# Sums of squares as rows in column groups, turned by transposes, in a two-block model on one core

## The chip, the core and the metric

The kernel runs on one core of one Trainium2 chip. Times are device microseconds of one execution. TensorE multiplies matrices into PSUM; VectorE, ScalarE and GpSimd work element by element; SyncE issues the DMAs. Each engine runs its own instructions in order and waits on semaphores.

## The reference

A first block (gated linear attention with grouped-query attention, a scan layer, two feed-forward layers) and a second block with a delta rule, latent attention and a mixture of experts, all in float32, for 256 context and 512 latent tokens of 1024 features. The two parts that the change touches, cut:

```python
# delta rule: gates of 8 heads in two directions, from 32 columns of the input projection
g = -jnp.exp(a_log) * jax.nn.softplus(alpha + dt_bias)
beta = jax.nn.sigmoid(beta_logit)
# latent attention: rms_norm(x, g) = x * rsqrt(mean(x * x) + EPS) * g
q = (rms_norm(c_q, q_a_norm_g) @ w_uq).reshape(b_, n_tok, MLA_HEADS, MLA_QK_DIM)
q = rms_norm(q, q_norm_g)                       # per head, over 128 + 64 features
kv = (rms_norm(c_kv, kv_a_norm_g) @ w_ukv).reshape(b_, n_tok, MLA_HEADS, MLA_NOPE + MLA_V)
k = rms_norm(jnp.concatenate([k_nope, k_pe], axis=-1), k_norm_g)
```

So the gates need a product of the tokens with 32 weight columns, and latent attention needs, for each token, the sum of squares over the 256 key/value features, the 64 rotary features, the 384 query features, and over each head's query.

## The kernel before

The program is a row of stages with a barrier of all engines between them. Inside a stage each engine has its own list of instructions, written out by hand in the order in which they are to run, with semaphores between the engines. There is no planner. Tokens lie in 6 tiles of 128 (two of context, four latent). `hT` holds the features on partitions, tokens along the row, in 8 slices (`KD`).

**Delta rule (`delta_mixer`).** Work goes in periods p (one head enters in each) of six steps n. In p = 0, TensorE projects the keys in step 0 (16 passes of 512 columns), the context's keys in step 1, then the gates' logits (`gate_logits`, L3609), the values in step 2 (`side("v")`, L3442), the cumulative sums of the gates (L3652, waits for `g_done`), the context's values in step 3, and the sums of squares of the keys (`ssk`, L3479). In `gate_logits` the tokens are the stationary operand (128 x 128) and the 32 gate columns `wab` the moving one: 6 tiles x 8 slices. The logits come out with tokens on partitions in `ps[:, 7]`. VectorE copies them (L3874), adds the bias, ScalarE does sigmoid (L3738), absolute value, exponential, logarithm (each with a table to load), VectorE ends with L3878 and L3879 (`g_done`). VectorE has the keys' convolution queued behind these, ScalarE has the first tap (L3683, which waits for the constants `const_in`) ahead of the gates.

**Latent attention (`mla`).** TensorE projects 8 units (keys/values, rotary key, query rank), ScalarE squares each (L4364), VectorE copies it out with its gain. Then TensorE sums the squares over the features, with the squares as the stationary operand and a column of ones (`one`) as the moving one: L4248 and L4249 for 6 tiles, L4254 for the four latent tiles. A sum comes out as one column, tokens on partitions. VectorE adds epsilon (L4491), ScalarE takes the root (L4368). Then come the rotary swap (L4258), the first keys (`keys(0)`, L4190), the second, the first values (L4201), and for each tile the turn of the scaled keys (`turn_keys`, L4211). ScalarE squares the keys of a tile at L4376 once the rotary key is rotated (`q_roped`), VectorE scales them at L4513.

The queries follow in 12 units (`lift`, L4180: six passes of 512 columns each). Behind each lift stand the sums of the unit before it (`sums`): four matmuls of one column (L4228) or, for a rotary pair, of two (L4231, with `half_ones`). Into three places the rotary swap is put, VectorE rotates (`rope`, L4480 to L4483). At the end VectorE gathers the sums (L4543 to L4545), ScalarE takes the root, and the attention itself begins with `qk(0)` and the maximum (L4560).

Each float32 matmul shows as two passes, each with its load of the stationary operand.

## Time and profile before

| | us |
|---|---|
| three runs | 4120.4, 4126.63, 4128.65 |
| median | 4126.63 |
| the profiled execution: time | 4120.5 |
| its span, first to last instruction | 4118.7 |

| engine | busy, share of the span |
|---|---|
| TensorE, matmuls | 3918.9 us, 95% |
| TensorE, loads | 2410.3 us, 59% |
| VectorE | 1656.0 us, 40% |
| ScalarE | 857.5 us, 21% |
| GpSimd | 680.1 us, 17% |

Busy time of matmuls counts pipelined passes until their modelled end. The table of stretches gives, for a part of the span, the busy time and the number of instructions of each engine and the mean granted clock of TensorE (PEclk: 1.00 is 2.4 GHz, 0.50 is 1.2 GHz).

### The profile page before, as it was taken

The numbers are of one execution on the slowest core, as the hardware profiler recorded it, in microseconds if no ns is written. First come the engines' busy times: TensorE is split into PE (matmuls) and PEld (weight loads), VectorE is DVE, ScalarE is ACT, GpSimd is POOL, SyncE is SP. The second block draws the span as 40 slices with busy tenths as digits, with TensorE's granted clock in tenths as the row PEclk, the third lists the DMA queues.
The fourth block names the chain that finished last, engine by engine and source line by source line (L and its number), as shares of the span: only waits on it lengthen the run. The fifth ranks groups of instructions, "written<-read, shape, count | busy, mean of one in ns | idle before, by whom it ended". The sixth has DMA issues, their size and how long they took to land. (4 is left out here: it accounts for less than half of the span.)

```text
span 4118.7 us, 51892 instructions
## 1 busy us (share of the span) xinstructions
PE 3918.9 (95%) x21121; PEld 2410.3 (59%) x21121; DVE 1656.0 (40%) x3076; ACT 857.5 (21%) x1680; POOL 680.1 (17%) x504
## 2 busy tenths in 40 slices
PE   7998899999999999999999999989999999999988
PEld 4565545555448666588845777767656545443333
DVE  2345343324764564443474656543244314111111
ACT  3224320000121333210113333331123201100000
POOL 0002212222420111032341423220003200000000
PEclk9999999999999999999999999999999998999999
DMA  5108611112441110164253111003300416999999
GB/s 179 41 1 286 219 41 62 62 62 100 171 129 57 47 31 26 62 255 165 92 177 68 27 32 29 22 33 113 117 1 1 164 44 256 405 421 422 422 421 372
DMA packets 323235, 580.09 MB, mean 141 GB/s; under 512 B 58828, under 2 KB 189228, under 8 KB 322360
## 3 DMA queue, kind: packets, MB, share of 16 engines
q1 hardware_dynamic: 323000, 576.77, 38.2%
q8 instruction: 170, 2.79, 0.3%
q14 instruction: 65, 0.53, 0.0%
HBM read 566.08 MB, written 10.63 MB: 140 GB/s over the span
## 5 line engine op out<-in xcount | busy, mean ns | idle before, releaser
L3442 PE MATMUL dn_ps<-room,dn_w 128*128 128x512 f32 (+1 forms) x616 | 230.8, 521 | 0.5 <-DVE dn_v_tok L3992 0.3
L974 PE MATMUL ffn_up_ps<-room 128*128 128x384 f32 (+1 forms) x704 | 203.9, 432 | 0.0
L974 PE MATMUL ffn_up_ps<-ffn_up_t,room 128*128 128x384 f32 (+1 forms) x704 | 196.7, 432 | 0.0
L5008 PE MATMUL experts_ps<-experts_ring,experts_xs 128*64 128x512 f32 (+1 forms) x768 | 162.4, 573 | 23.9 <-DMA experts_ring<-in_w_up 23.9
L2730 PE MATMUL hgrn_ps<-room,hgrn_w 128*128 128x512 f32 x372 | 170.4, 593 | 1.4 <-DVE hgrn_v L2985 0.9
L5008 PE MATMUL experts_ps<-experts_ring,room 128*64 128x512 f32 (+1 forms) x768 | 160.9, 570 | 8.7 <-DMA experts_ring<-in_w_up 8.1
L974 PEld LDWEIGHTS ffn_up_ps<-room 128*128 128x128 f32 x704 | 133.8, 190 | 55.7
L974 PEld LDWEIGHTS ffn_up_ps<-ffn_up_t,room 128*128 128x128 f32 x704 | 133.8, 190 | 55.7
L1060 DVE TENSOR_TENSOR room<-ffn_up_ps,room 128x384 f32<-128x384 f32 (+1 forms) x154 | 73.5, 489 | 222.2 <-PE ffn_up_ps L974 220.6
L5102 DVE TENSOR_TENSOR x_sb<-x_sb,experts_ps 128x512 f32<-128x512 f32 x56 | 38.5, 688 | 298.0 <-PE experts_ps L4943 298.0
L3442 PEld LDWEIGHTS dn_ps<-room,dn_w 128*128 128x128 f32 x616 | 113.0, 192 | 76.5 <-issue 67.0
L1249 PE MATMUL ffn_down_ps<-ffn_down_w_sums,ffn_w 128*128 128x512 f32 x330 | 151.7, 596 | 0.0
L5058 PE MATMUL experts_ps<-experts_ring,experts_hidT 128*64 128x512 f32 x616 | 136.9, 600 | 9.3 <-issue 5.2
L974 PE MATMUL ffn_up_ps<-room,ffn_w 128*128 128x384 f32 (+1 forms) x512 | 143.6, 434 | 0.0
L5008 PEld LDWEIGHTS experts_ps<-experts_ring,experts_xs 128*64 128x64 f32 x768 | 58.2, 140 | 129.0 <-issue 126.6
L664 PE MATMUL out_ps<-out_w,room 128*128 128x512 f32 x296 | 130.7, 600 | 0.8 <-ACT room L712 0.8
L974 PEld LDWEIGHTS ffn_up_ps<-room,ffn_w 128*128 128x128 f32 x512 | 96.9, 190 | 41.4 <-issue 1.1
L5008 PEld LDWEIGHTS experts_ps<-experts_ring,room 128*64 128x64 f32 x768 | 54.1, 139 | 110.2 <-issue 109.1
L1249 PEld LDWEIGHTS ffn_down_ps<-ffn_down_w_sums,ffn_w 128*128 128x128 f32 x330 | 63.5, 192 | 80.6 <-issue 79.4
L5058 PEld LDWEIGHTS experts_ps<-experts_ring,experts_hidT 128*64 128x64 f32 x616 | 51.1, 138 | 90.6 <-issue 90.4
L3829 POOL TENSOR_TENSOR dn_LT<-dn_W,cst 128x384 f32<-128x384 f32 x48 | 48.0, 1000 | 331.9 <-DVE dn_W L3915 294.8
L2730 PEld LDWEIGHTS hgrn_ps<-room,hgrn_w 128*128 128x128 f32 x372 | 65.8, 191 | 60.7 <-issue 59.4
(707 smaller groups left out, 7318.2 us busy)
## 6 DMA issues: line engine op xcount, KB each, us to landing
experts_ring<-in_w_gate SPq DMA_DIRECT2D x128, 704.0 KB, 15.3
experts_ring<-in_w_up SPq DMA_DIRECT2D x128, 704.0 KB, 17.0
experts_ring<-in_w_down SPq DMA_DIRECT2D x160, 512.0 KB, 14.1
att_wm<-in_mod_w SPq DMA_DIRECT2D x20, 2048.0 KB, 9.6
ffn_w<-in_ffn_w_down SPq DMA_DIRECT2D x37, 1024.0 KB, 4.9
ffn_up_wm<-in_ada_w SPq DMA_DIRECT2D x12, 2048.0 KB, 12.6
ffn_w<-in_ffn_w_up SPq DMA_DIRECT2D x22, 1024.0 KB, 7.6
ffn_front<-in_ffn_w_down SPq DMA_DIRECT2D x18, 1024.0 KB, 4.8
```

The costliest lines, as they stand in the source:

```text
L664: mm = nc.tensor.matmul(ps[:, u % BANKS, 0:wd], xT[:, k, t * P:(t + 1) * P], wt[:, j % ring, k, 0:wd], start=k == 0, stop=k == kt - 1)
L974: mm = nc.tensor.matmul(result(n, p), lhs[:, k, :], rhs[:, k, :], start=k == 0, stop=k == half - 1)
L1060: nc.vector.tensor_tensor(kept(n, to), result(n, p), kept(n, q), ALU.add).then_inc(done, 1)
L1249: mm = nc.tensor.matmul(result(p, prod), lhs, rhs, start=j == 0, stop=j == STEPS - 1)
L2730: mm = nc.tensor.matmul(ps[:, bank, :], weights(j, k)[:, piece * P:(piece + 1) * P], hT[:, k, CTX:], start=k == 0, stop=k == KD - 1)
L3442: mm = nc.tensor.matmul(out, ahead.tile[:, k, :] if k < by_ahead else wt[:, h % 2, piece, k, :], hT[:, k, tok], start=k == 0, stop=k == KD ...
L3829: nc.gpsimd.tensor_tensor(LT[:, :, :], W[:, h % 2, :, :], small(SMALL_HALVES + n + 1), ALU.mult).then_inc(S["lt_done"], 1)
L5008: mm = nc.tensor.matmul(ps[out_rows, 3 * n + c, 0:b - a], xs_now[:, j, at:at + SLOTS], ring[:, w_at + a:w_at + b], start=j == 0, stop=j == ...
L5058: mm = nc.tensor.matmul(ps[out_rows, 6 + half, :], hidT[:, f, out_rows], ring[:, w_at:w_at + 512], start=f == 0, stop=f == FT - 1)
L5102: nc.vector.tensor_tensor(dst, dst, ps[:, bank, :], ALU.add).then_inc(S["scatter_out"], 1)
```

## The change

The operands of the sums trade places. In latent attention the squares become the moving operand. The stationary one is a window of `marks`, 32 columns wide, that is one in the column of the head's row and zero elsewhere, so that each head's sum lands in its own row. Each token tile (or pair of tiles) has its own group of 32 output partitions. The sums come out as rows, with tokens along the row: three groups of 256 tokens for keys/values and rotary key, four of 128 for the queries' rank and for the queries themselves. The query sums of all 12 units add up in the same place. ScalarE (first sums) or VectorE (queries) copies the rows to SBUF, TensorE turns them by transposes, and VectorE reads them with tokens on partitions as before. The gates' logits are made in the same way: `wab` is stationary, three groups of 256 tokens, one ScalarE copy, two transposes set into the values' projection. The transposes of the first sums stand between the first and the second keys, and VectorE waits for them; the query rows are turned after the last rotary swap. GpSimd sets the marks with nine memsets in place of one, and the constant `half_ones` with its DMA goes.

Semaphore names, the width of `marks` and the loop over the constants' DMAs are left out here.

```diff
@@ -3328,13 +3328,16 @@
         wab = spare[:, 2 * (SPAN + GAP):][:, 0:KD * 4 * H].rearrange("p (k n) -> p k n", k=KD)
+        AB_GROUPS, AB_TOK = 3, 2 * P
+        AB_ROWS = AB_GROUPS * 4 * H
+        ab_rows = dec[0:AB_ROWS, 0:2, :].rearrange("p c i -> p (c i)")
         n_ahead = ahead.tile.shape[1]
...
@@ -3602,11 +3605,19 @@
             side_a = (None, "kc", "v", "vc", None, "kk")
-            def gate_logits():
+            def gate_rows():
+
                 pe.wait_ge(S["ab_in"], 16)
-                for c in range(TILES):
-                    for k in range(KD):
-                        mm = nc.tensor.matmul(ps[:, 7, c * 4 * H:(c + 1) * 4 * H], hT[:, k, c * P:(c + 1) * P], wab[:, k, :], start=k == 0, stop=k == KD - 1)
+                for k in range(KD):
+                    for n in range(AB_GROUPS):
+                        mm = nc.tensor.matmul(ps[n * 4 * H:(n + 1) * 4 * H, 6, 0:AB_TOK], wab[:, k, :], hT[:, k, n * AB_TOK:(n + 1) * AB_TOK], start=k == 0, stop=k == KD - 1)
+                mm.then_inc(S["ab_rows"], 1)
+
+            def gate_tokens():
+
+                pe.wait_ge(S["ab_rows_out"], 1)
+                for c in range(AB_TOK // P):
+                    mm = nc.tensor.transpose(ps[:, 7, c * AB_ROWS:(c + 1) * AB_ROWS], ab_rows[:, c * P:(c + 1) * P], ident[0:AB_ROWS, 0:AB_ROWS])
                 mm.then_inc(S["ab_mm"], 1)
@@ -3619,12 +3630,16 @@
                     side("q", hp, 0, KD // 2)
+                elif p == 0 and n == 2:
+                    side("v", hp, 0, 2)
+                    gate_tokens()
+                    side("v", hp, 2, KD)
                 else:
                 if p == 0 and n == 1:
-                    gate_logits()
+                    gate_rows()
                 if n == 0:
@@ -3774,6 +3789,9 @@
                     raw("kc", hp)
+                    if p == 0:
+                        act.wait_ge(S["ab_rows"], 1)
+                        nc.scalar.copy(ab_rows, ps[0:AB_ROWS, 6, 0:AB_TOK]).then_inc(S["ab_rows_out"], 1)
                     tap0("k", hp)
@@ -3871,7 +3889,7 @@
             dve.wait_ge(S["const_in"], CONSTS)
-            nc.vector.tensor_copy(ab[:, :, :].rearrange("p c j -> p (c j)"), ps[:, 7, 0:TILES * 4 * H]).then_inc(S["ab_out"], 1)
+            nc.vector.tensor_copy(ab[:, :, :].rearrange("p (n c) j -> p n c j", n=AB_GROUPS), ps[:, 7, 0:TILES * 4 * H].rearrange("p (c n j) -> p n c j", n=AB_GROUPS, j=4 * H)).then_inc(S["ab_out"], 1)
             dve.wait_ge(S["ab_out"], 1)
@@ -4119,7 +4137,19 @@

-        CONSTS = 16 * 12 + 1
+        CONSTS = 16 * 11 + 4
+        GROUP = P // 4
+        FIRST_GROUPS, FIRST_TOK = 3, 2 * P
+        FIRST_ROWS = FIRST_GROUPS * GROUP
+        kv_rows, cq_rows, q_rows = qn[0:FIRST_ROWS, 0, 0:FIRST_TOK], qn[:, 1, 0:P], cT[:, 0, 0:P]
+
+        def whole_mark(r, rows=slice(0, P)):
+
+            return marks[rows, 0, H - 1 - r:H - 1 - r + GROUP]
+
+        def pair_mark(r):
+
+            return marks[:, 1, 2 * H - 2 - r:2 * H - 2 - r + GROUP]

@@ -4223,12 +4253,9 @@
                 src = q_sq[:, ring_slot[u], :]
-                if what == "qn":
-                    for c in range(LATENT):
-                        mm = nc.tensor.matmul(ps[:, 6, c * H + n:][:, 0:1], src[:, c * P:(c + 1) * P], one[:, 2:3], start=True, stop=True)
-                else:
-                    for c in range(LATENT):
-                        mm = nc.tensor.matmul(ps[:, 6, (LATENT + c) * H + 2 * n:][:, 0:2], src[:, c * P:(c + 1) * P], one[:, 0:2], start=True, stop=True)
+                mark = whole_mark(n) if what == "qn" else pair_mark(H + 2 * n)
+                for c in range(LATENT):
+                    mm = nc.tensor.matmul(ps[c * GROUP:(c + 1) * GROUP, 6, 0:P], mark, src[:, c * P:(c + 1) * P], start=u == FIRST_Q, stop=u == len(units) - 1)
                 mm.then_inc(S["ss_mm"], 1)
@@ -4242,22 +4269,26 @@
             pe.wait_ge(S["squares"], sq_through[4])
-            for c in range(TILES):
-                tok = slice(c * P, (c + 1) * P)
-                for i in range(KC):
-                    nc.tensor.matmul(ps[:, 4, c:c + 1], sqc[:, i, tok], one[:, 2:3], start=i == 0, stop=i == KC - 1)
-                mm = nc.tensor.matmul(ps[:, 4, 8 + c:9 + c], kp[0:ROPE, 3, tok], one[0:ROPE, 2:3], start=True, stop=True)
+            for i in range(KC + 1):
+                for n in range(FIRST_GROUPS):
+                    tok = slice(n * FIRST_TOK, (n + 1) * FIRST_TOK)
+                    lhs, rhs = (whole_mark(0), sqc[:, i, tok]) if i < KC else (whole_mark(1, slice(0, ROPE)), kp[0:ROPE, 3, tok])
+                    mm = nc.tensor.matmul(ps[n * GROUP:(n + 1) * GROUP, 4, 0:FIRST_TOK], lhs, rhs, start=i == 0, stop=i == KC)
             mm.then_inc(S["ss_mm"], 1)
             pe.wait_ge(S["squares"], sq_through[7])
-            for c in range(LATENT):
-                for i in range(KQ):
-                    mm = nc.tensor.matmul(ps[:, 6, 16 + c:17 + c], sqq[:, i, c * P:(c + 1) * P], one[:, 2:3], start=i == 0, stop=i == KQ - 1)
+            for i in range(KQ):
+                for c in range(LATENT):
+                    mm = nc.tensor.matmul(ps[c * GROUP:(c + 1) * GROUP, 6, 0:P], whole_mark(0), sqq[:, i, c * P:(c + 1) * P], start=i == 0, stop=i == KQ - 1)
             mm.then_inc(S["ss_mm"], 1)
             keys(0)
+            pe.wait_ge(S["rows_out"], 2)
+            for c in range(FIRST_TOK // P):
+                nc.tensor.transpose(ps[:, 4, FIRST_TOK + c * FIRST_ROWS:FIRST_TOK + (c + 1) * FIRST_ROWS], kv_rows[:, c * P:(c + 1) * P], ident[0:FIRST_ROWS, 0:FIRST_ROWS])
+            nc.tensor.transpose(ps[:, 6, P:2 * P], cq_rows, ident).then_inc(S["first_turned"], 1)
             keys(1)
@@ -4277,6 +4308,8 @@
             swap_q(PAIRS - 1)
+            pe.wait_ge(S["q_rows_out"], 1)
+            nc.tensor.transpose(ps[:, 6, P:2 * P], q_rows, ident).then_inc(S["q_turned"], 1)

@@ -4393,6 +4426,10 @@
                 square(u)
+            act.wait_ge(S["ss_mm"], 1)
+            nc.scalar.copy(kv_rows, ps[0:FIRST_ROWS, 4, 0:FIRST_TOK]).then_inc(S["rows_out"], 1)
+            act.wait_ge(S["ss_mm"], 2)
+            nc.scalar.copy(cq_rows, ps[:, 6, 0:P]).then_inc(S["rows_out"], 1)
             root(1, sm[:, 1, 0:TILES], sm[:, 0, 0:TILES])
@@ -4441,7 +4478,13 @@
         def _(pool):
-            nc.gpsimd.memset(one[:, 2:3], 1.0).then_inc(S["const_in"], 1)
+            for n, part, value in ((0, slice(0, H - 1), 0.0), (0, slice(H - 1, H), 1.0), (0, slice(H, GROUP + H - 1), 0.0),
+                                   (1, slice(0, 2 * H - 2), 0.0), (1, slice(2 * H, GROUP + H - 1), 0.0)):
+                nc.gpsimd.memset(marks[:, n, part], value).then_inc(S["marked"], 1)
+            pool.wait_ge(S["marked"], 5)
+            for a in range(2):
+                for b in range(2):
+                    nc.gpsimd.memset(marks[a * ROPE:(a + 1) * ROPE, 1, 2 * H - 2 + b:2 * H - 1 + b], 1.0 if a == b else 0.0).then_inc(S["const_in"], 1)
             for u in range(len(unit_list)):
@@ -4487,16 +4530,20 @@
                 evacuate(u)
-            dve.wait_ge(S["ss_mm"], 1)
-            nc.vector.tensor_scalar(sm[:, 0, 0:TILES], ps[:, 4, 0:TILES], 1.0 / KV_RANK, EPS, ALU.mult, ALU.add).then_inc(S["small"], 1)
-            own(nc.vector.tensor_scalar(sm[:, 10, 0:TILES], ps[:, 4, 8:8 + TILES], 1.0 / MLA_DH, EPS, ALU.mult, ALU.add))
+            dve.wait_ge(S["first_turned"], 1)
+            by_group = ps[:, 4, FIRST_TOK:FIRST_TOK + 2 * FIRST_ROWS].rearrange("p (c n r) -> p n c r", c=2, n=FIRST_GROUPS)
+
+            def grouped(x):
+                return x.rearrange("p (n c) -> p n c", c=2)
+
+            nc.vector.tensor_scalar(grouped(sm[:, 0, 0:TILES]), by_group[:, :, :, 0], 1.0 / KV_RANK, EPS, ALU.mult, ALU.add).then_inc(S["small"], 1)
+            own(nc.vector.tensor_scalar(grouped(sm[:, 10, 0:TILES]), by_group[:, :, :, 1], 1.0 / MLA_DH, EPS, ALU.mult, ALU.add))
             dve.wait_ge(S["evac"], evac_through[4])
             own(nc.vector.scalar_tensor_tensor(sm[:, 11, 0:TILES], sm[:, 2, 0:TILES], 1.0 / MLA_DH, sm[:, 2, 0:TILES], ALU.mult, ALU.mult))
-            dve.wait_ge(S["ss_mm"], 2)
-            own(nc.vector.tensor_scalar(sm[:, 10, 8:8 + LATENT], ps[:, 6, 16:16 + LATENT], 1.0 / Q_RANK, EPS, ALU.mult, ALU.add))
+            own(nc.vector.tensor_scalar(sm[:, 10, 8:8 + LATENT], ps[:, 6, P:2 * P].rearrange("p (c r) -> p c r", r=GROUP)[:, :, 0], 1.0 / Q_RANK, EPS, ALU.mult, ALU.add))
             own(nc.vector.tensor_scalar(sm[:, 10, 8:8 + LATENT], sm[:, 10, 8:8 + LATENT], EPS, None, ALU.mult))
@@ -4540,8 +4587,11 @@
             HQ = LATENT * H
-            own(nc.vector.tensor_copy(sm[:, 4, 0:HQ], ps[:, 6, 0:HQ]))
-            own(nc.vector.tensor_tensor(sm[:, 3, 0:HQ], ps[:, 6, HQ:2 * HQ], sm[:, 4, 0:HQ], ALU.add))
+            nc.vector.tensor_copy(q_rows, ps[:, 6, 0:P]).then_inc(S["q_rows_out"], 1)
+            dve.wait_ge(S["q_turned"], 1)
+            q_sums = ps[:, 6, P:2 * P].rearrange("p (c r) -> p c r", r=GROUP)
+            own(nc.vector.tensor_copy(by_tile(sm[:, 4, 0:HQ]), q_sums[:, :, 0:H]))
+            own(nc.vector.tensor_tensor(by_tile(sm[:, 3, 0:HQ]), q_sums[:, :, H:2 * H], by_tile(sm[:, 4, 0:HQ]), ALU.add))
             nc.vector.scalar_tensor_tensor(by_tile(sm[:, 3, 0:HQ]), by_tile(sm[:, 3, 0:HQ]), 1.0 / MLA_DH, over_heads(sm[:, 10, 8:8 + LATENT], LATENT), ALU.mult, ALU.add).then_inc(S["small"], 1)
```

## Rows read from the trace of the kernel before

**Rows 1.** Stretches around the gates; the columns are named in the first line.

```profile
core 0: us, PE busy (x) PEld busy (x) DVE busy (x) ACT busy (x) POOL busy (x), PEclk, DMA share, GB/s
...
2210.10:2226.20 16.10, 16.10 (x98) 16.06 (x97) 0.00 (x0) 4.09 (x5) 0.50 (x1) 0.66 0.81 143
...
2242.00:2246.20 4.20, 4.20 (x6) 1.66 (x7) 3.95 (x7) 2.05 (x3) 3.44 (x2) 0.59 0.23 69
```

**Rows 2.** Timeline around the gates: start, duration, engine, line, operation, idle before it.

```profile
2210.12 16.14 PEld L3609 LDWEIGHTS dn_ps<-x_sb,room 128*128 128x128 f32 x96
...
2220.29 0.94 ACT L3683 ACTIVATE dn_kT<-x_sb,dn_taps 128x772 f32<-128x772 f32 x1 [9.38 <-DMA dn_dtb<-in_dt_bias]
...
2222.77 1.28 ACT L3738 ACT_TABLE_LOAD   x1
...
2227.12 0.28 ACT L3738 ACTIVATE dn_beta<-dn_ab 128x96 f32<-128x96 f32 x1 [3.06 <-DVE dn_gx L3876]
...
2231.17 0.26 DVE L3879 SCALAR_TENSOR_TENSOR dn_g<-dn_g,dn_al 128x96 f32<-128x96 f32 x1
...
2234.47 1.43 PE L3652 MATMUL dn_ps<-dn_g,cst 128*128 128x48 f32 x12
...
2240.07 1.50 PE L3479 MATMUL dn_ps<-cst,dn_sq 128*128 128x1 f32 x12 [0.64 <-ACT dn_sq L3704]
```

**Rows 3.** Stretches of latent attention's first sums and of what follows them.

```profile
2979.40:2991.10 11.70, 11.70 (x62) 11.24 (x61) 0.99 (x3) 2.09 (x3) 0.00 (x0) 0.66 0.00 0
2991.10:2998.40 7.30, 7.30 (x12) 3.17 (x13) 2.67 (x7) 0.00 (x0) 0.00 (x0) 0.60 0.01 3
```

**Rows 4.** Timeline from the first sums to the first turn of keys.

```profile
2979.87 0.50 PE L4248 MATMUL mla_ps<-mla_one,mla_probs 128*128 128x1 f32 x4
...
2991.16 2.05 PE L4258 MATMUL mla_ps<-mla_kr,cst 128*128 128x512 f32 x2
...
2993.36 0.69 DVE L4480 TENSOR_TENSOR mla_probs<-mla_ps,mla_sin 128x512 f32<-128x512 f32 x1 [6.99 <-PE mla_ps L4258]
...
2998.57 1.02 ACT L4376 ACTIVATE mla_probs<-mla_ps 128x1024 f32<-128x1024 f32 x1 [12.03 <-PE mla_ps L4190]
...
3002.02 1.22 DVE L4513 TENSOR_TENSOR mla_probs<-mla_ps,mla_sm 128x1024 f32<-128x1024 f32 x1
...
3005.84 1.09 PE L4211 MATMUL mla_ps<-cst,mla_probs 128*128 128x128 f32 x8
```

**Rows 5.** Timeline of the query units and of their end.

```profile
3054.41 0.95 PE L4228 MATMUL mla_ps<-mla_one,mla_probs 128*128 128x1 f32 x8
...
3057.88 0.95 PE L4231 MATMUL mla_ps<-mla_one,mla_probs 128*128 128x2 f32 x8
...
3091.34 0.19 DVE L4543 COPY mla_sm<-mla_ps 128x32 f32<-128x32 f32 x1
...
3098.41 0.96 DVE L4560 TENSOR_REDUCE mla_st<-mla_ps 128x1 f32<-128x768 f32 x1 [3.21 <-PE mla_ps L4298]
```

**Rows 6.** Timeline of the modulation's matmuls in column groups and their neighbours.

```profile
1777.85 1.89 PE L974 MATMUL ffn_up_ps<-room 128*128 128x256 f32 x8
1779.67 3.68 PE L1005 MATMUL ffn_up_ps<-ffn_up_wm,conditions 128*2 128x128 f32 x128
1783.28 3.72 PE L974 MATMUL ffn_up_ps<-room,ffn_w 128*128 128x256 f32 x16
1786.84 3.62 PE L974 MATMUL ffn_up_ps<-ffn_up_t,room 128*128 128x256 f32 x16
1790.29 1.89 PE L974 MATMUL ffn_up_ps<-room 128*128 128x256 f32 x8
...
323.75 1.64 PEld L2176 LDWEIGHTS att_ps<-att_wm,conditions 128*2 128x2 f32 x64 [1.47 <-DMA att_wm<-in_mod_w]
...
325.61 1.16 PEld L2226 LDWEIGHTS att_ps<-even_raw 64*128 64x128 f32 x8 [0.22 <-issue]
```

**Rows 7.** Loads, grouped by line and shape: busy us, mean ns of one.

```profile
L3442 PEld LDWEIGHTS dn_ps<-room,dn_w 128*128 128x128 f32 x616 | 113.0, 192 | 76.5 <-issue 67.0 <-DVE dn_neg_m L3969 0.5 <-DVE dn_v_tok L3992 0.4
L1005 PEld LDWEIGHTS ffn_up_ps<-ffn_up_wm,conditions 128*2 128x2 f32 x768 | 19.4, 85 | 3.6 <-issue 3.0
```

More of the change, by code:

```diff
@@ L3211, in rope_tables @@
         pick[2 * c:2 * c + 2, c, :] = two.T
-    tables = {"rope_cos": np.cos(ang), "rope_sin": np.sin(ang), "rope_swap": swap, "half_ones": two, "pick_rows": pick}
+    tables = {"rope_cos": np.cos(ang), "rope_sin": np.sin(ang), "rope_swap": swap, "pick_rows": pick}
     return {name: np.ascontiguousarray(t.astype(np.float32)) for name, t in tables.items()}
@@ L3336, in delta_mixer @@
         ps = stack.enter_context(nc.psum_tensor(f"{tag}_ps", [P, 8, 512], F32))
-        block, S = stack.enter_context(phase(nc, tag, "const_in", "ab_in", "triangle_in", "w_in*6", "ab_mm", "ab_out", "gates", "gates_act", "g_done", "sums_mm", "sums_exp", "neg_done",
+        block, S = stack.enter_context(phase(nc, tag, "const_in", "ab_in", "triangle_in", "w_in*6", "ab_rows", "ab_rows_out", "ab_mm", "ab_out", "gates", "gates_act", "g_done", "sums_mm", "sums_exp", "neg_done",
                                              "side", "y_mm", "d_mm", "dt_mm", "ks_mm", "tr_mm", "su_mm", "o_mm",
@@ L4058, in mla @@
         sm = sb("sm", 12, 48)
-        one = sb("one", 3)
+        marks = sb("marks", 2, P // 4 + H - 1)
         st = sb("st", 2, 4, 2)
@@ L4075, in mla @@
         ps = stack.enter_context(nc.psum_tensor(f"{tag}_ps", [P, 8, 512], F32))
-        block, S = stack.enter_context(phase(nc, tag, "const_in", "up_in*2", "mm_done", "squares", "evac", "v_out", "ss_mm", "small", "root", "swapped", "rotated",
+        block, S = stack.enter_context(phase(nc, tag, "const_in", "up_in*2", "mm_done", "squares", "evac", "v_out", "ss_mm", "rows_out", "first_turned", "q_rows_out", "q_turned", "marked", "small", "root", "swapped", "rotated",
                                              "kr_turned", "kr_copied", "v_mm", "k_mm", "k_squared", "k_sum", "k_mean", "k_root", "k_scaled", "k_turned", "k_out", "kp_out", "q_roped", "scores", "top_done", "max_done", "exp_done", "inverted",
@@ L4108, in _ @@
                 sp.dma_start(cols[rows, GAIN_KP:GAIN_KP + 1], k_gain[NOPE:].rearrange("(p a) -> p a", a=1)).then_inc(S["const_in"], 16)
-            for dst, src in ((cos, "quarter_cos"), (sin, "quarter_sin"), (swap, "quarter_swap"), (one[:, 0:2], "half_ones")):
-                sp.dma_start(dst if src in ("quarter_swap", "half_ones") else dst[:, :], I[src]).then_inc(S["const_in"], 16)
+            for dst, src in ((cos, "quarter_cos"), (sin, "quarter_sin"), (swap, "quarter_swap")):
+                sp.dma_start(dst if src == "quarter_swap" else dst[:, :], I[src]).then_inc(S["const_in"], 16)
             kv = w_ukv.rearrange("(k p) (h f) -> p k h f", p=P, h=H)
```

## The prediction

> **What bounds the kernel now.** I read the table of busy shares first: TensorE is busy in almost the whole span, every other engine in less than half of it, so what counts is TensorE's time in its own program order, wherever no other engine holds it up. Then I looked for the lines that the diff removes and found each in the timeline, and I read the granted clock around them in the table of stretches. Three places come out.
>
> The gates' logits: 96 passes (48 matmuls, each two passes in float32) between 2210.1 and 2226.2 us [rows 2]. The reader is to see the granted clock beside it: 0.66 in that stretch, that is, it falls from 2.4 to 1.2 GHz while these passes run, whose moving operand is 32 columns wide [rows 1].
>
> Latent attention's first sums: 36 + 24 passes with one moving column from 2979.87 us to the swap at 2991.16 us [rows 4], 11.3 us. The clock again falls under them (0.66) and stays down over the dense passes behind them (0.60) [rows 3].
>
> The query sums: eight passes of one or two moving columns between each two lifts. From 3054.41 to 3057.88 us one period takes 3.47 us [rows 5]. Its lift is six passes of 512 columns. A pass of 256 columns takes 0.216 us: sixteen of them lie between 1786.84 and 1790.29 us [rows 6]. So 512 columns take 0.43, the lift 2.59, and the sums 0.88 us.
>
> **What a group of columns costs.** The kernel already has such matmuls: the modulation writes four groups of output partitions, each matmul with 128 moving columns. In the gate and up projections 128 such passes go from first load to the next line's first load in 3.61 us, in the attention stage 64 in 1.86 us [rows 6]. The difference of 64 passes is 1.75 us, 27 ns a pass or 0.109 us for a round of four, which is what one pass of 128 columns takes alone (half of 0.216). So four groups run side by side. The rest of 3.61 us is 0.11. Entering costs 0.10 more (eight passes before it take 1.82 instead of 1.73 us) and leaving 0.11 (sixteen take 3.56 instead of 3.45). So a block is its rounds plus 0.32 us of switching. The new stationary operand is 32 columns wide, not 2. A load of 2 columns takes 85 ns, one of 128 192 ns [rows 7]; I take about 110 ns by their spacing, which shows at a block's head only (0.03), since four loads of 32 columns are what one load of 128 is, and those keep up with 128 moving columns today. If they did not overlap the streams, each round would be twice as long; I keep that for a rival.
>
> The Trainium skill, page "TensorEngine Tiling (Array Packing)", section Key Properties, says that a change of the tiling mode drains TensorE, and this change puts 24 such changes among the query lifts. By that rule, the trace agrees: the 0.32 us is such a drain. The page gives no price of its own. The Trainium skill, page "TensorE: Matmul & The Clock Gate", section on packing small matmuls, gives 2.38 times for three column tiles, where the rounds here are counted as three at once. By it the two blocks with three groups would take a quarter longer, 1.2 us in all, and 0.9 of that is in the gates, where it is hidden.
>
> **Part 1, gates.** 24 matmuls, 48 passes of 256 columns in three groups: 16 rounds x 0.216 + 0.32 = 3.8 us in place of 16.1. TensorE comes to the values' projection at 2213.9 instead of 2226.2 us. But who waits for the gates? ScalarE cannot start its part before the convolution's taps are in: it waits for that DMA until 2220.29 us, then loads a table until 2224.05 us [rows 2]. The chain from its sigmoid at 2227.12 to the end of the logarithm's last step on VectorE at 2231.43 us is 4.31 us. In the new order the logits are there at about 2216 (rows out by ScalarE, two transposes inside the values' projection), so the sigmoid starts at 2224.05 and the gates are done at 2228.4, 3.1 us earlier. TensorE has finished the values by 2213.9 + 6.9 + 0.4 = 2221.2 and now waits for the gates until 2228.4; 12.3 us of saved passes become about 7 us of idle time. Behind it stand the cumulative sums, the context's values and the sums of the keys' squares, which before started at 2240.07 us, held up by ScalarE's square [rows 2]. That square hangs on the convolution, which VectorE has queued behind the gates, so it moves by 3.1 us. TensorE wakes up at half clock: 12 passes of 0.2 and 16 of 0.43 (twice their time at full clock) put it at 2237.7 us, at full clock at 2234.5; the square is ready at 2237.0. So this part gives 2.4 to 3.1 us there. What the clock does next is open: before, the queries' passes ran at 0.59 [rows 1], about 1.7 us lost. If that goes, it is 4.8; if another 1.7 comes, 0.7. I take 3.0. ScalarE's new copy lies in a stretch where it only waits for the taps.
>
> **Part 2, first sums.** Keys' and values' sums: 9 matmuls, 18 passes of 256 columns, six rounds of 0.216 = 1.29 us. The queries' rank: 12 matmuls, 24 passes, six rounds of 0.109 = 0.65. Switching 0.32 and 0.2 for the two changes between them (64 rows for the rotary part, then four groups; an estimate from the 0.10 of entering). Together 2.5 in place of 11.3: 8.8 us. If the clock stays up, the ten passes of the swap and the first keys take 4.6 us to their reader instead of 7.41 (2991.16 to 2998.57) [rows 4]: 2.8 us more. Against it, three transposes ahead of the second keys: 0.5 us with their gaps. Together 11.1 us.
>
> That is TensorE's order alone. The new waits: ScalarE's two copies stand ahead of its root, TensorE's transposes behind the first keys; the copies end by about 2983, the transposes stand at 2986.7, so nobody waits. VectorE's first small steps now wait for the transposes (2987.2), and the rotation of the rotary keys is queued behind them. Its three operations of 0.69 us [rows 4] end at 2989.9, and only then may ScalarE square the keys. From there to the scaled keys it is 4.67 us (2998.57 to 3003.24), so 2994.6. TensorE reaches the turns at 2987.2 + 6.9 + 0.6 = 2994.7, against 3005.84 before. There is next to no slack, and a microsecond may be lost here. Bounds for this part: 9 (loads and chain dearer) and 12.
>
> **Part 3, query sums.** 2 rounds x 0.109 + 0.32 + 0.03 = 0.57 in place of 0.88 us, 0.31 x 11 = 3.4 us. The twelfth block is covered by VectorE's rotation. Bounds: 0 (a block costs what it did) and 6 (switching costs next to nothing). At the end VectorE copies the rows out, TensorE turns them and VectorE goes on: about 0.8 us later than at 3091.34, and the rotation of the last pair behind it. Before the first maximum VectorE idles 3.21 us [rows 5], which hides it; without that cover it would cost the 0.8.
>
> **The rest.** Nine memsets in place of one on GpSimd, and eleven constants instead of twelve from the queue of SyncE, lie at the stage's start, under the first projections: 0. The stages follow each other with barriers and the experts' weights are requested after them, so the gain is kept.
>
> Sum: 3.0 + 11.1 + 3.4 = 17.5 us. The profiled execution took 4120.5 us (span 4118.7, 1.8 around it), near the fastest of the three; the median is 6.1 above. Against the execution it gives 4103, against the median 4126.63 - 17.5 = 4109.
>
> **Rivals.**
> (a) The gates give nothing, because TensorE idles and the clock takes back the rest: 14.5 us gained, 4112. For it: the new idle time of 7 us; against it: before, this stretch has half clock too.
> (b) The drains eat part 3 (a block costs 0.88): 14.1 gained, 4112.5. For it: VectorE and ScalarE are not the limit, so each drain is on the path; against it: the 0.32 measured between dense blocks [rows 6]. This is the mechanism the tiling page warns of.
> (c) With 32 columns to load, groups do not run side by side. First sums: 18 x 0.216 + 24 x 0.109 + 0.5 = 7.0, so 4.5 less than forecast. A query block is 8 x 0.109 + 0.35 = 1.2, 0.3 worse than before. The gates' logits take 10.7 us and still end near 2221, which hides it. 3.0 + 6.6 - 3.6 = 6.0 gained, 4120.6, within what can't be told from no change.
> (d) Slower: each group's matmul must drain the array before the next, so that a query block of eight passes costs 0.4 us each, 3.2 us: 2.3 x 11 = 26 lost, and the first sums with 42 x 0.4 = 17 us lose 5.5 more. Half of that comes back at the clock and the gates, 6: about 25 slower, 4152. It decides from 2.2 us a block on. Against it: 27 ns a pass in 64 and in 128 passes [rows 6].
>
> **How the numbers follow.** Forecast 0.65, (a) 0.13, (b) 0.12, (c) 0.08, (d) 0.02. A measurement of this kernel tells about 0.2%, 8.3 us, from no change. Faster by more than that: the first three, 0.90; within it: 0.08; slower: 0.02. The range takes the bounds of the parts (0.7 to 4.8, 9 to 12, 0 to 6), about 9.7 to 22.8 gained, and a few microseconds for the runs, which spread over 8: 4101 to 4118.
>
> **What would show it.** In the profile after: 48 passes of the rows within 4 us of 2210; TensorE idle before the cumulative sums, with the gates done near 2228; the granted clock at 1.00 through the first sums; the scaled keys ready when TensorE arrives; a query period of 3.16 us. The prediction fails if a query block stays near 0.9 us, if the clock falls after the first sums, or if TensorE waits for the scaled keys.

## The result and the profile after

| | median us | lowest to highest | runs |
|---|---|---|---|
| before | 4119.42 | 4114.13 to 4128.65 | 6 |
| after | 4097.82 | 4090.99 to 4105.98 | 6 |

The ratio is 0.9948, with a 95% interval of 0.9938 to 0.9958: 21.6 us faster. The forecast was 4109, 17.5 below a median of 4126.63, with a range of 4101 to 4118; the time fell out of that range at the lower end. The profiled execution of the changed kernel took 4105.98 us, the slowest of its six. So its span (4104.2) against that of before (4118.7) shows less than the runs do.

The page of the changed kernel, busy times:

```profile
PE 3905.2 (95%) x21061; PEld 2383.8 (58%) x21061; DVE 1656.4 (40%) x3077; ACT 857.2 (21%) x1683; POOL 679.7 (17%) x512
```

TensorE has 13.7 us less to do; the other engines are as they were.

**Gates.** Stretches of the changed kernel: the logits' rows, the idle time ahead of the cumulative sums, from these to the keys' sums of squares, and what follows:

```profile
2209.20:2212.83 3.63, 3.63 (x49) 1.88 (x49) 0.00 (x0) 0.37 (x1) 0.00 (x0) 1.00 0.76 5
2220.20:2228.10 7.90, 0.01 (x1) 0.01 (x1) 1.18 (x5) 7.77 (x12) 0.50 (x1) 0.78 0.79 237
2228.10:2236.30 8.20, 8.20 (x29) 7.17 (x29) 6.14 (x4) 4.43 (x5) 4.34 (x2) 0.58 0.00 0
2236.30:2250.00 13.70, 12.54 (x49) 7.23 (x49) 11.77 (x14) 7.02 (x8) 6.02 (x3) 1.00 0.15 40
```

Its timeline there:

```profile
2209.24 3.17 PEld L3613 LDWEIGHTS dn_ps<-room,x_sb 128*32 128x32 f32 x48 [0.33 <-issue]
...
2214.65 0.33 PE L3620 MATMUL dn_ps<-cst,dn_dec 96*128 96x96 f32 x2
...
2223.72 0.28 ACT L3753 ACTIVATE dn_beta<-dn_ab 128x96 f32<-128x96 f32 x1
...
2227.78 0.26 DVE L3897 SCALAR_TENSOR_TENSOR dn_g<-dn_g,dn_al 128x96 f32<-128x96 f32 x1
...
2228.09 2.79 PE L3667 MATMUL dn_ps<-dn_g,cst 128*128 128x48 f32 x12 [7.93 <-DVE dn_g L3897]
...
2235.25 0.85 ACT L3719 ACTIVATE dn_sq<-dn_kT 128x772 f32<-128x772 f32 x1
...
2236.30 1.40 PE L3482 MATMUL dn_ps<-cst,dn_sq 128*128 128x1 f32 x12
```

The reader is to see four things. The 48 passes take 3.6 us instead of 16.1 [rows 1]. TensorE then idles 7.9 us, since the gates are ready only at 2228.04. It comes back at 1.2 GHz (0.58 in the third stretch). And from the keys' sums of squares on the clock is 2.4 GHz (1.00), where before it was down again for part of the stretch behind them [rows 1].

**First sums and first keys:**

```profile
2974.50:2977.00 2.50, 2.50 (x44) 1.19 (x43) 0.75 (x1) 0.96 (x2) 0.00 (x0) 1.00 0.00 0
2977.00:2989.00 12.00, 12.00 (x39) 5.45 (x35) 6.07 (x14) 3.87 (x7) 0.00 (x0) 1.00 0.01 1
```

```profile
2974.61 1.06 PE L4276 MATMUL mla_ps<-mla_probs,mla_marks 128*32 128x256 f32 x12
...
2976.16 0.86 PE L4281 MATMUL mla_ps<-mla_probs,mla_marks 128*32 128x128 f32 x24
...
2976.95 1.12 PE L4285 MATMUL mla_ps<-mla_kr,cst 128*128 128x512 f32 x2
...
2981.35 0.33 PE L4290 MATMUL mla_ps<-cst,mla_qn 96*128 96x96 f32 x2
...
2983.42 0.69 DVE L4526 TENSOR_TENSOR mla_kr<-mla_probs 128x512 f32<-128x512 f32 x1
...
2984.21 1.02 ACT L4409 ACTIVATE mla_probs<-mla_ps 128x1024 f32<-128x1024 f32 x1 [1.98 <-DVE mla_kr L4526]
...
2987.66 1.22 DVE L4560 TENSOR_TENSOR mla_probs<-mla_ps,mla_sm 128x1024 f32<-128x1024 f32 x1
...
2989.11 1.09 PE L4241 MATMUL mla_ps<-cst,mla_probs 128*128 128x128 f32 x8
```

The sums take 2.34 us to the swap instead of 11.29, at full clock; swap to first turn takes 12.15 us instead of 14.68 [rows 3, 4]. The keys are scaled at 2988.88 and TensorE arrives at 2989.11, so no wait has come in.

**Query units:**

```profile
3034.30 0.42 PE L4258 MATMUL mla_ps<-mla_probs,mla_marks 128*32 128x128 f32 x8
3034.66 2.84 PE L4210 MATMUL mla_ps<-mla_cqT,mla_big 128*128 128x512 f32 x6
3037.43 0.43 PE L4258 MATMUL mla_ps<-mla_probs,mla_marks 128*32 128x128 f32 x8
```

A period is 3.13 us (3034.30 to 3037.43) instead of 3.47 [rows 5].

### The profile page after: what moved, and what is told of

Read it like the earlier page. It is cut to its first block and busy times, and to the rows that moved or that the text cites. A ratio compares the mean times of both kernels' runs of the same rounds, so it can differ in the third digit from the quotient of the medians.

```text
span 4104.2 us, 51781 instructions
## 1 busy us (share of the span) xinstructions
PE 3905.2 (95%) x21061; PEld 2383.8 (58%) x21061; DVE 1656.4 (40%) x3077; ACT 857.2 (21%) x1683; POOL 679.7 (17%) x512
## 5 line engine op out<-in xcount | busy, mean ns | idle before, releaser
L5058 PEld LDWEIGHTS experts_ps<-experts_ring,experts_xs 128*64 128x64 f32 x768 | 59.2, 140 | 126.8 <-issue 123.8
## 6 DMA issues: line engine op xcount, KB each, us to landing
experts_ring<-in_w_down SPq DMA_DIRECT2D x160, 512.0 KB, 13.7
```

The source lines that it names most:

```text
L5058: mm = nc.tensor.matmul(ps[out_rows, 3 * n + c, 0:b - a], xs_now[:, j, at:at + SLOTS], ring[:, w_at + a:w_at + b], start=j == 0, stop=j == ...
```

## The experiments

The kernels were run in three groups, each on a chip of its own, and beside each group the kernel before was timed on the same chip: 4119.65 us (33 runs) beside the first four kernels, 4120.62 (22) beside the next four, 4118.84 (16) beside the last four.

### One part at a time

Each of three kernels is the kernel before with one part of the change; a fourth is the kernel before itself, timed as if it were a new one. A theory or a rival below is named as in the expectation that stands ahead of the run.

```diff
 # gates alone: the hunks in delta_mixer
-                    gate_logits()
+                    gate_rows()
 # first sums alone: rows, copies and transposes of L4276 to L4291, queries as before
-                    nc.tensor.matmul(ps[:, 4, c:c + 1], sqc[:, i, tok], one[:, 2:3], ...)
+                    mm = nc.tensor.matmul(ps[n * GROUP:(n + 1) * GROUP, 4, 0:FIRST_TOK], lhs, rhs, ...)
 # queries alone
-                        mm = nc.tensor.matmul(ps[:, 6, c * H + n:][:, 0:1], src[:, c * P:(c + 1) * P], one[:, 2:3], ...)
+                    mm = nc.tensor.matmul(ps[c * GROUP:(c + 1) * GROUP, 6, 0:P], mark, src[:, c * P:(c + 1) * P], ...)
```

Gates alone. 

> The kernel before with the gates' part alone. Theory A, the parts add up and each is worth what its own stretch of the trace shows: the delta rule's stage 4.2 us shorter (3.0 if the clock falls again at the queries' passes), the other stages as before; by the clock about 4 us faster, ratio 0.9990. Rival B, the gates are only worth something together with the rest: 0 to 1 us in the stage. The whole change was 21.6 us faster by its medians and 17.6 by the stages of its trace; A puts the difference down to runs, B to one of the parts.

First sums alone. 

> Latent attention's first sums alone as rows in groups. Theory A: from the first sum to the first turn of keys 14.5 us instead of 26.0, so 11.4 us, ratio 0.9972. Rival B (the part is worth more by the clock than the trace shows, because a clock that stays up helps beyond its stretch): over 15 us faster.

Query sums alone. 

> The queries' sums alone as rows in groups. Theory A: a period of lift and sums 3.13 us instead of 3.47, 3.7 us over the eleven, less up to 1 us at the turn at the end (a transpose at half clock ahead of the first scores): 3 us faster, ratio 0.9993. Rival B: over 7 us faster, or none at all if the drains cost more where the rest is unchanged.

The kernel before. 

> The kernel before, not changed at all. Theory A: run to run the times spread over 10 us, since the granted clock falls in other places of each execution, and medians of five such runs differ by up to 4 us (ratio 0.999 to 1.001). Rival B (runs of one kernel agree, so a difference of 4 us between two medians has a cause in the program): within 1 us.

| kernel | median us | ratio | 95% interval |
|---|---|---|---|
| gates | 4115.89 | 0.9988 | 0.9978 to 0.9997 |
| first sums | 4112.03 | 0.9980 | 0.9969 to 0.9991 |
| query sums | 4117.00 | 0.9992 | 0.9983 to 1.0001 |
| the kernel before | 4117.60 | 1.0000 | 0.9990 to 1.0010 |

In microseconds of 4119.5: 4.9, 8.2 and 3.3, together 16.5, each known to about 4 and the sum to about 7. All three came out as their theory A has it, within that. The gates' interval only just leaves out no change, and the queries' does not; their stretches are clearer. From the delta rule's first matmul to the solve's first the gates alone make 59.2 us into 54.2. The unchanged kernel shows what single executions scatter: 4109.83 to 4127.47 over eleven, with a median 2.05 us below that of the 33 beside it, as its theory A has it.

### The whole change again, with padding, without column groups, and with the waits moved

The whole change again. 

> The whole change once more, with more runs. Theory A (what it is worth is what the changed stretches of the traces show, 17 to 18 us, and the 21.6 of the first six runs had luck in it): ratio 0.9957, 18 us faster. Rival B (21.6 us is its true worth, and 4 us come from somewhere that the stretches don't show): ratio 0.9948 again, with an interval that leaves 0.9957 out.

It took 4096.56 us, ratio 0.9943 (0.9929 to 0.9957). Theory A's 0.9957 lies at the very end of the interval, so that the median speaks for rival B, but does not leave A out.

The first sums padded: ten dense matmuls of 512 columns (twenty passes, no output of theirs is used) ahead of the rotary swap.

```diff
             pe.wait_ge(S["evac"], evac_through[4])
+            keep_busy(nc, ps[:, 7, :].rearrange("p (a n) -> p a n", a=4), ident, ident.unsqueeze(1).broadcast_to([P, 4, P]), 10)
             nc.tensor.matmul(ps[:, 7, :], swap, kr...)
```

> The whole change, with ten dense matmuls of 512 columns (the identity, result unused) between the first sums and the rotary swap, so that this stretch takes as long as before but with a busy array. Theory A, the first sums gave by two means, 8.4 us by fewer passes and 2 by a clock that stays up behind them: the stretch to the swap 10.9 us again, the stretch from the swap to the first turn 12.15 us as in the change, against 13.3 to 14.7 with the sums of before; 9 us slower than the whole change. Rival B, the clock is off the path there, the stretch behind the swap is what the new order of waits makes it: no difference to be seen at the clock, which would be 1.00 in both, and the stretch from the swap longer than 12.15 or the stretch before it not 10.9.

It took 4112.73 us, ratio 0.9980 (0.9970 to 0.9991). Stretches of the padded kernel, from its sums to the swap and on to the first turn:

```profile
2978.10:2989.20 11.10, 11.10 (x63) 5.05 (x63) 0.75 (x1) 2.51 (x4) 0.00 (x0) 1.00 0.00 0
2989.20:3001.30 12.10, 12.10 (x37) 5.46 (x35) 6.07 (x14) 2.46 (x5) 0.00 (x0) 1.00 0.00 1
```

The padded sums are as long as those of before (11.03 against 11.29 us from the first sum to the swap), but TensorE is fed with wide operands, and behind them the clock stays at 1.00: swap to turn takes 12.06 us, not 14.68. So the part's gain behind the swap (2.5 us in the profiled executions) is the clock, and comes from what runs in the sums and not from how long they take: theory A. The other 8.9 us (11.29 less 2.34) are the sums themselves; part of these too is clock, since they ran at 0.66 before [rows 3] and run at 1.00 now. By the medians the padding costs 16 us, where theory A had 9 and its twenty passes take 8.6. The two ratios (15 us apart, known to about 7) leave room for that, and the open point below comes back to it.

The query sums without column groups: one matmul of 512 columns a unit, and four transposes at the end instead of one.

```diff
-                for c in range(LATENT):
-                    mm = nc.tensor.matmul(ps[c * GROUP:(c + 1) * GROUP, 6, 0:P], mark, src[:, c * P:(c + 1) * P], start=u == FIRST_Q, stop=u == len(units) - 1)
+                mm = nc.tensor.matmul(ps[0:GROUP, 6, :], mark, src, start=u == FIRST_Q, stop=u == len(units) - 1)
```

> The whole change, but the queries' sums in one group of 32 rows: per unit one matmul of 512 moving columns (two passes) in place of four of 128 (eight passes), turned by four transposes. It does the same sums. Theory A, four groups run side by side and the rest of a block is the switch: two passes of 0.43 and 0.32 make 1.2 us, the period 3.8 us in place of 3.13, 7 us slower than the whole change. Rival B, a block's cost is a price for each pass or the drain, not the streaming: two passes cost no more than eight, the period stays at 3.13 us or below.

It took 4107.97 us, ratio 0.9964 (0.9950 to 0.9978). Its timeline:

```profile
3036.12 1.05 PE L4257 MATMUL mla_ps<-mla_probs,mla_marks 128*32 128x512 f32 x2
3037.10 2.84 PE L4210 MATMUL mla_ps<-mla_cqT,mla_big 128*128 128x512 f32 x6
3039.87 1.04 PE L4257 MATMUL mla_ps<-mla_probs,mla_marks 128*32 128x512 f32 x2
```

The period is 3.75 us, 0.62 more than with groups and 0.28 more than before; theory A had 3.8. From the first lift to the last rotary swap it is 48.74 us, against 41.93 with groups and 45.67 before. In the query units, trading the operands alone makes the kernel slower: two passes of 512 tokens past 32 columns take 1.05 us in these rows, the two past 128 columns of the rotary swap 1.12 us above. There, only four streams side by side turn it into a gain. The first sums and the gates were not run without groups.

The waits moved: VectorE convolves the first keys before the last two steps of the gates, TensorE projects the context's values ahead of the wait for `g_done`, and four dense passes stand ahead of the last rotary swap.

```diff
                     side("v", hp, 2, KD)
+                    side("vc", hp)
...
+            for j in range(1, DN_CONV):
+                conv("k", 0, j)
             dve.wait_ge(S["gates_act"], 5)
...
             sums(len(units) - 1)
+            keep_busy(nc, ps[:, 4, :].rearrange("p (a n) -> p a n", a=4), ident, ident.unsqueeze(1).broadcast_to([P, 4, P]), 2)
             swap_q(PAIRS - 1)
```

> The whole change, and three moves in the stretches where engines wait now: VectorE does the first keys' convolution while ScalarE makes the gates (it was queued behind them), TensorE projects the first context values before it waits for the gates, and two dense matmuls (identity, unused) stand ahead of the last rotary swap. Theory A, after the change the way to the first ssk is the chain gates, convolution, silu, square and no longer TensorE: ssk 3 us sooner, and the attention's first scores up to 1.5 us sooner if the clock stays up; 4 us faster than the whole change, ratio to before 0.9946 or so. Rival B, TensorE's own order is the path there all the same: no change at ssk, and the added matmuls only cost.

It took 4100.72 us, ratio 0.9951 (0.9937 to 0.9965), not distinguishable from the whole change and not the 4 us faster that theory A had. Its timeline and stretches behind the gates:

```profile
2233.33 2.80 PE L3668 MATMUL dn_ps<-dn_g,cst 128*128 128x48 f32 x12 [5.23 <-DVE dn_g L3912]
...
2237.88 0.85 ACT L3707 ACTIVATE dn_kT<-dn_kT 128x772 f32<-128x772 f32 x1
2238.76 0.85 ACT L3720 ACTIVATE dn_sq<-dn_kT 128x772 f32<-128x772 f32 x1
...
2239.66 2.72 PE L3482 MATMUL dn_ps<-cst,dn_sq 128*128 128x1 f32 x12 [3.54 <-ACT dn_sq L3720]
```

```profile
2233.30:2239.60 6.30, 2.80 (x12) 2.63 (x12) 0.00 (x0) 4.54 (x6) 2.92 (x2) 0.50 0.00 0
2239.60:2246.00 6.40, 6.09 (x16) 4.15 (x17) 3.29 (x8) 3.98 (x6) 2.44 (x2) 0.50 0.01 3
2246.00:2260.00 14.00, 13.10 (x41) 6.42 (x39) 10.42 (x10) 4.25 (x5) 5.03 (x4) 0.99 0.14 36
```

The square of the keys now ends 6.3 us after the gates (2239.61 against 2233.27), in the changed kernel 8.1, since ScalarE no longer waits for the convolution. But the context's values no longer cover the time until then. TensorE idles twice, 5.2 and 3.5 us, and stays at 1.2 GHz (0.50) up to 2246, through the sums of squares and most of the projection behind them, where the changed kernel has 1.00. From the stage's first matmul to the sums of squares it took 36.42 us against 37.54 in the changed kernel, 1.1 less where 3 were expected; from there to the solve's first (L3496) 20.35 against 17.24. Together that is 56.77 against 54.78. Less waiting at one place was paid back at the clock. The dense passes ahead of the last swap show nothing: the stretch behind it took 14.4 us at 1.00, as in three traces without them.

### Three pairs and the whole

The parts alone summed to 16.5 us and the whole was measured at 21.6 and 24. So all three pairs were run, with the whole once more.

> The whole change once more, beside its three pairs. The parts alone gained 4.9 (gates), 8.2 (first sums) and 3.3 us (query sums) by their ratios, 16.5 in all, each known to about 4 us; the whole gained 21.6 and 24. Theory 1, the parts simply add and the whole was measured somewhat high: about 4102, ratio 0.9958. Theory 2, the whole is worth more than its parts alone: about 4097, ratio 0.9945 again.

> First sums and query sums as rows, the gates as before. Theory 1 (parts add): 11.5 by the parts' ratios to 14.5 by the forecast's own sum, ratio 0.9972 to 0.9965. Theory 2 (these two parts, in one stage, lift each other by the clock): 19 us or more, ratio 0.9954 or below, and the whole then stands only some 3 us below it.

> Gates and first sums as rows, the query sums as before. Theory 1: 13 to 14 us gained, ratio about 0.9967, and the whole is 3.4 us below it, which is what the query units' own rows give (eleven times 0.34). Theory 2: more than 18 us, or the whole more than 6 us below it.

> Gates and query sums as rows, the first sums as before. Theory 1: 6.4 to 8 us gained, ratio about 0.9982, and the whole is 10 to 12 us below it (the forecast priced the first sums at 11.1). Theory 2: the whole is 15 us or more below it.

| kernel | median us | ratio | 95% interval |
|---|---|---|---|
| whole | 4096.52 | 0.9945 | 0.9931 to 0.9958 |
| first sums and queries | 4107.49 | 0.9970 | 0.9959 to 0.9982 |
| gates and first sums | 4103.07 | 0.9960 | 0.9947 to 0.9972 |
| gates and queries | 4111.39 | 0.9979 | 0.9970 to 0.9987 |

All eight combinations are now there, so each part can be taken in four settings. By the ratios, in us of 4119.5 (whole: mean of its three ratios, 22.5):

| part | alone | beside the one | beside the other | beside both | mean | by the traces |
|---|---|---|---|---|---|---|
| gates | 4.9 | 8.2 (first sums) | 5.4 (queries) | 10.1 | 7.2 | 4.8 |
| first sums | 8.2 | 11.5 (gates) | 9.1 (queries) | 13.9 | 10.7 | 10.2 |
| queries | 3.3 | 3.7 (gates) | 4.1 (first sums) | 6.0 | 4.3 | 3.7 |

A mean is known to about 3 us (half-widths near 0.001 of 4119.5, eight ratios in two fours, taken as independent). The last column is the difference of stretches between fixed instructions. From the delta rule's first matmul to the solve's first (L3496 in the changed kernel) it is 59.16 to 59.20 us in the five traces with the old logits and 53.88 to 54.86, mean 54.4, in the eight with the new ones (the kernel with the waits moved, 56.77, left out). From the first sum to the first turn it is 14.50 us in all the traces with the new sums that are not padded; in the five with the old ones 25.97 (the profiled execution of before), 24.45, 24.40, 24.34 and 24.29, mean 24.7. From the first lift to the last rotary swap it is 45.67 and 41.93.

The pairs do not settle between the two theories. The whole itself came out where theory 2 had it, at 0.9945, with theory 1's 0.9958 at the end of its interval. First sums with queries gave 11.3 us by the medians, as theory 1 had it, and their interval leaves out the 19 of theory 2. But the whole stands 11.0 us below them, 6.6 below gates with first sums and 14.9 below gates with queries, each more than theory 1 had. None of the intervals, of parts, pairs or whole, excludes that the means simply add. The three ratios of the whole together, as independent, put it at 22.5 us give or take 3, which is more than the 16.5 of the parts alone; but that sum is itself known to about 7 only. The traces' column adds to 18.7; the 3.5 us that the runs show beyond it are about what a mean is known to.

Part of it has a place. Stretches from the last rotary swap to the third `qk` in the changed kernel, in the whole change as run last, and before:

```profile
3071.00:3088.70 17.70, 14.40 (x47) 7.18 (x47) 8.34 (x20) 4.78 (x9) 2.62 (x1) 0.81 0.00 0
```

```profile
3070.90:3085.30 14.40, 11.08 (x47) 5.98 (x47) 8.37 (x20) 4.77 (x9) 2.63 (x1) 1.00 0.00 0
```

```profile
3091.40:3107.40 16.00, 12.66 (x46) 6.73 (x46) 8.19 (x19) 4.76 (x9) 2.63 (x1) 0.89 0.00 1
```

The last swap in the timelines of the first two:

```profile
3070.98 1.86 PE L4264 MATMUL mla_ps<-x_sb,cst 128*128 128x512 f32 x2 [1.84 <-DVE x_sb L4526]
```

```profile
3070.93 1.10 PE L4264 MATMUL mla_ps<-x_sb,cst 128*128 128x512 f32 x2 [1.84 <-DVE x_sb L4526]
```

The first two of the three stretches are the same program, 3.3 us apart, and the whole difference is the granted clock behind the 1.84 us in which TensorE waits for the rotation. Of the six traces that have both the new first sums and the new queries' sums in groups, four took 14.4 us here, one 16.1 and one (the profiled execution) 17.7. Of the seven that lack one of the two or both, one took 14.3, two 16.0 and four 17.6 to 17.8. The run without groups, which is in neither count, took 14.8. That is a tendency in few traces and no more.

## Why the prediction failed

The direction, the mechanism and the order of the parts were right; the time was not. Two steps failed. Of the 11.3 us between the forecast (4109.1) and the result (4097.8), 7.2 are the base (4126.63 against 4119.42) and 4.1 the gain (21.6 against 17.5). By the traces the gates give 1.8 more than their term and the queries 0.3, the first sums 0.9 less; the 2.9 us that remain are not placed by any trace.

**The base.** "Against the execution it gives 4103, against the median 4126.63 - 17.5 = 4109." The three runs shown had a median of 4126.63, but 77 executions of the kernel before have 4119.66, with 4112.1 to 4130.5 at the ends and five at 4126.6 or more. The profiled execution (4120.5) was the better base, and with it the same sum gives 4103. The range had the same fault: it allowed "a few microseconds for the runs" around a median that was itself 7 us off. From 4119.66 its lower end would have been about 4094, and would have held 4096.6, the median of 17 executions of the whole change. The gain of 21.6 lies within the 9.7 to 22.8 that the parts were given.

**The gates' term.** "I take 3.0" was too small. The stretch up to the keys' sums of squares is 37.54 us against 40.14: 2.6, within the 2.4 to 3.1 worked out. What was left open, "if that goes, it is 4.8", is what happened. From there to the solve it is 17.24 to 17.34 us in the eight new traces and was 19.04 in that of before, at 1.00 instead of 0.91. Three of the five old traces lost these 1.7 us behind the sums of squares, two ahead of them (41.82 us up to the sums and 17.34 behind); none was spared the loss, and the two stretches together are 59.2 in all five. The upper bound was right and the middle was taken without a reason to prefer it. What makes the loss go with the idle time is not shown; that it goes, a row of first sums with queries, which has the old gates, and one of the whole change show:

```profile
2240.40:2259.40 19.00, 17.84 (x56) 9.23 (x56) 13.71 (x17) 8.16 (x10) 7.47 (x5) 0.91 0.20 53
```

```profile
2238.60:2255.90 17.30, 16.14 (x59) 8.60 (x58) 13.67 (x17) 8.33 (x10) 7.46 (x5) 1.00 0.23 61
```

The other steps, against what was measured:

- Gates' rows in 3.8 us: 3.6; the quarter more for three groups that the prediction also worked out (it would make 4.7 us) does not show. Sigmoid at 2224.05 and gates done at 2228.4: 2223.72 and 2228.04, but in a stage that began 1.17 us earlier (2198.76 against 2199.93), so by the stage both are 0.8 us late. TensorE idle about 7 us: 7.9. The chain that was named (taps, table load, sigmoid, logarithm) is the one that set the time. One sum of it is wrong without effect: at full clock the passes behind the gates would end at 2233.1, not 2234.5, and the square at 2237.0 is later than either.
- First sums in 2.5 us: 2.34. Clock worth 2.8: 2.5 in the profiled pair, and with the transposes' 0.5 added back 3.0; against the five old traces together (13.95 us from swap to turn) 1.8 and 2.3. First turn at 2994.7 from a first sum at 2979.87, that is 14.8 us: 14.50. The term of 11.1 is right against that one execution (11.5), a microsecond too high against the five old traces together (10.2), because the profiled execution had lost more to the clock there than the other four. A trace of one execution prices a clock loss as it fell that time.
- VectorE's rotation "queued behind" the transposes, "next to no slack": the keys were scaled 0.23 us before TensorE came, so the slack was there and no larger.
- A query block of 0.57 us: 0.54 by the same measure (period less lift, 3.13 - 2.59). Period 3.16: 3.13. From the first lift to the last swap 3.74 us gained instead of 3.4. A load of 32 columns, taken at 110 ns: 108. The switch between a dense block and four groups costs here what it did around the modulation [rows 6].
- The end of the queries, hidden behind 3.21 us of VectorE's idle time: it still idles 1.79 us before the first maximum. The transpose lies on TensorE's path for 0.2 us.
- Memsets and constants at nothing: from the stage's first matmul to the first sum it is 51.63 to 51.73 us with or without them.

The rivals. (a) said that the clock takes back what the gates gave: the opposite happened, it gave 1.75 more; gates alone are faster, if by the runs only just (interval to 0.9997), and in their stretch by 5.0 us. (b), the drains eat part 3, is excluded by the period. By the Trainium skill, page "TensorEngine Tiling (Array Packing)", section Key Properties, a change of tiling mode drains TensorE; the trace agrees that a change costs something, with the 0.32 us in it, and the 0.54 us block against 0.22 us for two rounds of 128 columns is that price once more. That the price is a drain, as the prediction says, no run shows by itself. (c) is excluded by 48 passes in 3.6 us and by the run without groups: had the groups run one after the other, the period would have been about 3.8, as it is there (3.75). (d) likewise.

## What to carry to other kernels

A sum over partitions costs a stationary load per 128 tokens if the data is stationary; as the moving operand it costs its columns. Price both before trading. In the query units, whose loads took 192 ns each at full clock, the trade paid only with several groups of output partitions streaming side by side, after a fixed price for each block of grouped passes between dense ones (0.32 us; 0.34 us a block were left as gain). Elsewhere it may pay without groups: the prediction's own rival (c) has the first sums at 7.0 us so, an estimate that no run tested, against 11.3 before. Where narrow passes stood, read the granted clock behind them too: about a fifth of what the first sums gained came after they were over. And take the base of a forecast of half a per cent from all executions that are shown, the profiled one among them: three runs of a kernel whose executions scatter by 4 us either way put it 7 us off.

## What the runs showed that was not expected

- Two executions of one program differ in places, not evenly. The same 47 passes behind a wait of 1.84 us took 14.40 and 11.08 us of busy time, at a granted clock of 0.81 and 1.00. The delta rule's stage behind L3496 took 545.6 to 553.0 us in fourteen traces in which its instructions are the same; in the pair before and after the stretches agree to 0.1 us up to the last one, where the clock is 0.95 and 0.94:

```profile
2700.00:2808.10 108.10, 95.41 (x788) 69.20 (x787) 35.92 (x93) 27.10 (x71) 11.09 (x10) 0.95 0.12 41
```

```profile
2694.40:2803.20 108.80, 96.02 (x788) 71.36 (x786) 36.01 (x93) 27.05 (x71) 11.07 (x10) 0.94 0.12 40
```

- An idle wait ahead of a stretch does not fix its clock: after 7.9 us of idle TensorE ran 8.2 us at 0.58 and then at 1.00 throughout, while the old order, busy with narrow passes in place of the idle time, had 0.91 from the keys' sums to the solve in three of its five traces (in the other two the loss lay ahead of the sums). With two shorter waits of 5.2 and 3.5 us the clock was 0.50 over the 12.7 us behind the first of them, the second wait among them.
- The gain of the whole change beyond the traces' 18.7 us (22.2 by the runs) is left open. The padding and the run without groups point the same way: they cost 16.2 and 11.4 us by the medians (15 and 9 by the ratios, each known to 7 or 8), 8.6 and 6.8 in their own stretches. The traces show no sign of a part at work far from its own place. What is left of the span outside of the four stretches named above (gates, first sums, queries, and from the last swap to the third `qk`) is 3965.3 to 3975.3 us in the fourteen traces: 3971.9 and 3970.4 in the two of the kernel before, 3975.3, 3966.4 and 3969.7 in the three of the whole change, 3974.6 and 3973.7 in the padded kernel and the one without groups. Scatter of this size in the rest is enough for the open 3.5 us, but that it made them is not shown.
